# Block boundaries of a three-layer transformer kernel: transposing x before its norm, and projecting one token tile at a time

## The chip, the cores and the metric

The kernel runs on one core of a Trainium2 chip. The metric is the device time of one execution, in microseconds (us): the median of several runs. Five engines work side by side, each through its own instructions in order, and wait for each other by semaphores: TensorE (PE in the profile) multiplies matrices and writes to PSUM, VectorE (DVE) and ScalarE (ACT) work element by element, GpSimd (POOL) does little here, and SyncE (SP) issues the loads.

## The reference, cut to what matters

The input x has 256 tokens of 1024 features, in fp32. Two layers (an even and an odd one) come first, each a mixer and an MLP, and then one hybrid layer.

```python
def rmsnorm(x, g):
    y = xf * lax.rsqrt(jnp.mean(xf * xf, axis=-1, keepdims=True) + EPS)
    return (y * g.astype(jnp.float32)).astype(x.dtype)

def sq_relu_mlp(h, w1, w2):
    return jnp.square(jax.nn.relu(h @ w1)) @ w2

    for l in range(DEPTH):                       # DEPTH = 2
        h = rmsnorm(x, g[0])
        y = even_mixer(...) if l % 2 == 0 else odd_mixer(...)     # each begins with h @ w_in
        x = x + rmsnorm(y, g[1])
        h = rmsnorm(x, g[2])
        x = x + rmsnorm(sq_relu_mlp(h, mlp_w1[l], mlp_w2[l]), g[3])

    # hybrid layer: first operations
    shift, scale, gate = jnp.split(jax.nn.silu(c) @ w_ada + b_ada, 3, axis=-1)
    h = rms_norm(x, g_pre) * (1 + scale[:, None, :]) + shift[:, None, :]
    ... = jnp.split(h @ w_in, cuts, axis=-1)
```

So there are four places where one block's output passes through an rmsnorm, is added to x, and x passes through the next rmsnorm (with a bias at the fourth) into the next block's first projection. They are called boundaries here: 1 before the first MLP, 2 before the odd mixer, 3 before the second MLP, 4 before the hybrid layer.

## The kernel before

Everything is held in SBUF except the weights, which stream through in 150 tiles of 1 MB (128 partitions x 2048 fp32). `plan_tiles` lists them in the order of use. SyncE loads each into one of three buffers `raw`; a buffer is loaded again once its tile has been split. Each tile is split into two parts of a reduced fp32 format, so that three fast matmuls give an fp32 product: ScalarE casts it to `w_hi` (line 968) and VectorE writes the rest, `raw - w_hi`, to `w_lo` (line 1322). Three slots of `w_hi`/`w_lo` hold split tiles; a slot is taken again when TensorE has used its tile. Activations are split in the same way: `h_hi`/`h_lo` for a normed input, `f_hi`/`f_lo` for the inner MLP activation. TensorE's lines 464 to 466 are the three products.

The order of every engine's work is the order in which its program is written. ScalarE and VectorE run ahead of TensorE by a count: `split_until(past(name, 2))` (or `ahead(name)`) means "split all tiles up to two beyond this group, then go on". Six tiles per MLP (`ada`) are not split but summed on VectorE with a per-partition factor (lines 1313 to 1317), in place of their split.

Projections from x come in two kinds. Feature-major (`project_feature_major`): a stationary block of the weights, the moving operand `h` of 256 tokens, output with features on the partitions, 96 matmuls of 128x256 for one group of 512 columns. Token-major (`project_token_major`): `h` is stationary. Outputs go to one of two PSUM pairs `lin0`/`lin1` (1024 columns each), which take turns by a list (`plan_lin`). Row-wise sums (the last matmul of a block) go to `acc` (2048 columns: two token tiles of 1024 features). Of these sums the last two weight tiles are done together, token tile 0 first.

At a boundary `residual` runs on ScalarE and VectorE after `split_until(LAST[name] + 1)`, one token tile of 128 tokens at a time: ScalarE squares the block's output (line 987) and takes the root (983); VectorE takes the mean (1339), multiplies by the gain row (1380), takes the reciprocal (1343) and updates x (1387). Then ScalarE squares the new x, takes the root, and VectorE scales an identity matrix by 1/norm (1349). TensorE turns x by a matmul of x with that diagonal (`norm_in`, line 553), so that x is transposed and normed at once. When both token tiles are turned, `to_h` multiplies by the gain: ScalarE writes `h_hi` (1008) and VectorE `h_lo` (1361, with a bias 1364 and 1365) in pieces of 128x256, and the first projection starts.

After boundaries 1 and 3 the MLP's first projection `up_0` is read by ScalarE (relu, line 1029), squared on ScalarE (1033, `f_hi`) and VectorE (1586, 1588, `f_lo`), while TensorE does `up_1`; then `down_0` is summed. After boundary 2 the first projection `mq` is copied (1089) and passes through a four-tap convolution on VectorE (1625, 1627), and a small projection `mrowg` of gate rows feeds a chain of small operations (1656 to 1665). After boundary 4 `dk` goes the same way: copy, convolution, silu (1144), square (1205), and then a sum on TensorE (767).

## Time and profile before

| | us |
|---|---|
| median of 3 runs | 1030.27 (1027.41 to 1030.48) |
| span of the profiled execution | 1026.5 |
| TensorE busy | 953.2 (93%) |
| VectorE busy | 632.9 (62%) |
| ScalarE busy | 495.2 (48%) |
| loaded from HBM | 163.60 MB, 160 GB/s over the span |

The span is what the profiler saw from the first to the last instruction. The execution's own time is not listed apart from the three runs; they are 0.9 to 4.0 us above the span. A median 3.8 us above the span is the relation used below.

How to read the rows further down: a row of a timeline gives the start (us from the span's start), the duration of the merged piece, the engine, the line of the kernel, the operation and its operands with their shapes, and in brackets the idle time before it and whose result ended that idle time. "PE" rows overlap, since matmuls are pipelined: 128x256 matmuls that last 0.28 start 0.12 apart, 128x512 ones 0.23 apart.

### The profile page before, as it was taken

The page shows a single profiled execution, that of the slowest core. Times are in us where ns is not written, and L with a number is a line of the kernel's source. Part 1 is how long each engine was busy: PE and PEld are TensorE (multiplying, and loading weights), DVE is VectorE, ACT ScalarE, POOL GpSimd, SP SyncE. Part 2 cuts the span into 40 slices and gives each one's busy share as a digit, 9 for nine tenths or more (in the row PEclk, how much of TensorE's full clock was granted, in tenths as well). Part 3 has the DMA queues.
Part 4 walks back from the last instruction along what each step waited for, and adds up shares of the span by engine and source line. Part 5 has one row for each costly group of instructions (what it writes and reads, how often), then busy time and mean ns, then how long its engine had stood idle before and what let it go on. Part 6 is the DMA issues. An engine that isn't in the chain of part 4 may idle for free.

```text
span 1026.5 us, 13530 instructions
## 1 busy us (share of the span) xinstructions
PE 953.2 (93%) x5794; PEld 853.5 (83%) x5794; DVE 632.9 (62%) x738; ACT 495.2 (48%) x604; POOL 28.0 (3%) x21
## 2 busy tenths in 40 slices
PE   6999978989999997998889999999799999989897
PEld 6998867789999996976769999998698998877776
DVE  4678644667656656685557666655758673345655
ACT  6554534564444445435545444444555743237433
POOL 0000000000000000000000000000000232100000
PEclk9999989999999999998898999999799899999999
DMA  8545412536666543343334765665233242222431
GB/s 327 186 165 188 147 75 82 205 145 259 233 220 232 205 164 144 129 159 135 111 141 147 281 232 205 237 242 180 87 137 111 96 164 80 85 103 83 164 124 41
DMA packets 23755, 165.51 MB, mean 161 GB/s; under 512 B 2640, under 2 KB 2896, under 8 KB 4368
## 3 DMA queue, kind: packets, MB, share of 16 engines
q1 hardware_dynamic: 22176, 159.39, 42.6%
q0 software_dynamic: 1088, 4.46, 1.1%
q8 instruction: 45, 0.74, 0.3%
q10 hardware_dynamic: 432, 0.81, 0.2%
q14 instruction: 14, 0.11, 0.0%
HBM read 163.60 MB, written 1.05 MB: 160 GB/s over the span
## 4 chain that ended last, share of the span: by engine, by line
PE 64%; DVE 14%; ACT 7%; issue 2%; DVEq 0%; ACTq 0%
PE lin L464 11%; PE lin L465 11%; PE lin L466 11%; PE acc L464 7%; PE acc L465 7%; PE acc L466 7%; DVE w_lo L1322 3%; PE acc L571 2%; DVE arena L1627 1%; ACT arena L987 1%; ACT w_hi L968 1%; PE acc L846 1%; PE acc L843 1%; DVE h_lo L1361 1%; PE acc L834 1%
## 5 line engine op out<-in xcount | busy, mean ns | idle before, releaser
L1322 DVE TENSOR_TENSOR w_lo<-raw,w_hi 128x2048 fp32r<-128x2048 f32 x138 | 318.1, 2317 | 147.5 <-ACT w_hi L968 147.1
L968 ACT CAST w_hi<-raw 128x2048 fp32r<-128x2048 f32 x138 | 261.8, 1906 | 175.7 <-PE lin L466 96.8
L464 PE MATMUL lin<-h_hi,w_hi 128*128 128x256 f32 x864 | 252.2, 292 | 11.4 <-DVE h_lo L1361 5.9
L465 PE MATMUL lin<-h_lo,w_hi 128*128 128x256 f32 x864 | 250.1, 289 | 0.0
L466 PE MATMUL lin<-h_hi,w_lo 128*128 128x256 f32 x864 | 249.9, 289 | 0.0
L464 PEld LDWEIGHTS lin<-h_hi,w_hi 128*128 128x128 f32 x864 | 171.6, 199 | 13.5 <-DVE h_lo L1361 6.9
L465 PEld LDWEIGHTS lin<-h_lo,w_hi 128*128 128x128 f32 x864 | 172.0, 199 | 0.4
L466 PEld LDWEIGHTS lin<-h_hi,w_lo 128*128 128x128 f32 x864 | 171.6, 199 | 0.0
L464 PE MATMUL lin<-w_hi,h_hi 128*128 128x512 f32 x272 | 110.1, 405 | 6.4 <-DVE h_lo L1361 2.7
L464 PE MATMUL acc<-w_hi,f_hi 128*128 128x512 f32 x288 | 112.4, 390 | 0.9 <-DVE w_lo L1322 0.9
L465 PE MATMUL acc<-w_lo,f_hi 128*128 128x512 f32 x288 | 112.2, 390 | 0.0
L466 PE MATMUL acc<-w_hi,f_lo 128*128 128x512 f32 x288 | 112.1, 389 | 0.0
L465 PE MATMUL lin<-w_lo,h_hi 128*128 128x512 f32 x272 | 107.3, 395 | 0.0
L466 PE MATMUL lin<-w_hi,h_lo 128*128 128x512 f32 x272 | 107.1, 394 | 0.0
L464 PEld LDWEIGHTS lin<-w_hi,h_hi 128*128 128x128 f32 x272 | 52.1, 191 | 18.5 <-issue 4.6
L464 PEld LDWEIGHTS acc<-w_hi,f_hi 128*128 128x128 f32 x288 | 54.1, 188 | 12.5 <-issue 1.7
L466 PEld LDWEIGHTS acc<-w_hi,f_lo 128*128 128x128 f32 x288 | 54.1, 188 | 11.4
L465 PEld LDWEIGHTS acc<-w_lo,f_hi 128*128 128x128 f32 x288 | 54.1, 188 | 10.6
L466 PEld LDWEIGHTS lin<-w_hi,h_lo 128*128 128x128 f32 x272 | 51.9, 191 | 11.3
L465 PEld LDWEIGHTS lin<-w_lo,h_hi 128*128 128x128 f32 x272 | 52.0, 191 | 10.0
L1089 ACT ACTIVATE arena<-lin 128x1024 f32<-128x1024 f32 x23 | 23.6, 1025 | 55.3 <-PE lin L466 55.2
L464 PE MATMUL acc<-w_hi,h_hi 128*128 128x512 f32 x112 | 44.2, 395 | 2.6 <-DVE arena L1538 1.6
(295 smaller groups left out, 1092.6 us busy)
## 6 DMA issues: line engine op xcount, KB each, us to landing
raw<-in_weights SPq DMA_DIRECT2D x150, 1024.0 KB, 4.8
rowbuf<-in_rows POOLq DMA_DIRECT2D x6, 512.0 KB, 3.8
x<-in_x_in SPq DMA_DIRECT2D x2, 512.0 KB, 4.5
arena<-in_const_even POOLq DMA_DIRECT2D x1, 1024.0 KB, 11.0
out<-x SPq DMA_DIRECT2D x2, 512.0 KB, 2.6
cst<-in_const ACTq DMA_DIRECT2D x1, 576.0 KB, 9.3
msk<-in_masks POOLq DMA_DIRECT2D x1, 256.0 KB, 6.8
colbuf<-in_cols ACTq DMA_DIRECT2D x1, 151.0 KB, 5.8
```

What stands on the lines that cost most here:

```text
L464: pe.matmul(dst, st_hi, mv_hi, start=first, stop=False)
L465: pe.matmul(dst, st_hi, mv_lo, start=False, stop=False)
L466: return pe.matmul(dst, st_lo, mv_hi, start=False, stop=last)
L571: mm = pe.matmul(dst[:, at:at + width], pt(h, s, t), v(h, s), start=(s == 0), stop=(s == t))
L834: mm = pe.matmul(acc[:, i * P:(i + 1) * P], at("am", P, (l % 2) * 1024 + i * P), at("X", P, i * P), start=True, stop=True)
L843: pe.matmul(acc[:, 1024 + i * P:1024 + (i + 1) * P], at("Y", P, i * P), at("Pm", P, i * P), start=True, stop=True)
L846: mm = pe.matmul(acc[:, i * P:(i + 1) * P], at("Pm", P, i * P), at("Y", P, i * P), start=True, stop=True)
L968: act.copy(w_hi[:, o % SPLIT, :], raw[:, j % RAW, :]).then_inc(hi_done, 1)
L987: act.activation(arena[:, at:at + 512], src, ACT.Square, accum_out=stat[:, 2 * t + c:2 * t + c + 1]).then_inc(ss_ready, 1)
L1089: act.activation(dst.rearrange("p (t c) -> p t c", t=TT) if len(dst.shape) == 2 else dst, pair(name)[:, :].rearrange("p (t c) -> p t c", t ...
L1322: dve.tensor_tensor(w_lo[:, o % SPLIT, :], r, w_hi[:, o % SPLIT, :].bitcast(F32), ALU.subtract).then_inc(tile_split, 1)
L1361: ins = dve.scalar_tensor_tensor(lo, src, gain(k), hi, ALU.mult, ALU.subtract)
```

## The change

1. **x is transposed unscaled.** The 16 matmuls with the scaled diagonal (`norm_in`) go. TensorE transposes x itself (`turned`), four 128x128 pieces after each half of the update of x. Those of token tile 0 stand ahead of the last six matmuls of the block's sum (`between`; not at boundary 4), which for token tile 1 is done tile by tile instead of column half by column half.
2. **The norm factor follows the projection.** At boundaries 1 to 3 `h` is x times the gain only. The projection's output is multiplied by 1/norm when it is read: as ScalarE's `scale` for token-major outputs, and for feature-major ones by a row of factors on all partitions (`every`), made by one matmul of ones with a diagonal (line 656 of the new kernel). The MLP's relu of `up_1` to `up_7` moves from ScalarE to VectorE for that. At boundary 4, which has a bias, x is scaled by VectorE before the transpose.
3. **The first projection is token-major, one token tile at a time** (`lead`): 96 matmuls of 128x256 into `acc`, each token tile as soon as its `h` is there. ScalarE reads it (`lead_out`), and TensorE transposes it back with eight 128x128 transposes (`lead_turned`), in the MLP in the middle of `up_1`, else after the small gate projection.
4. **Two more slots for split tiles** in the free part of the work area, for the MLPs' tiles and `mq`, `dk` (`plan_slots`), and three tiles instead of one are split ahead of the boundary's own work (`split_until(past(name, 3))`).
5. `h` is written in pieces of 128x128 (one token tile) instead of 128x256.

```diff
+            def lead(name, names, done, scaled=False):
+                def products(i, t, ks):
+                    hi, lo = split_tile(FIRST[name] + i)
+                    at = t * 512 + i * 256
+                    for k in ks:
+                        if i == 0 and k == 0:
+                            after(ht_ready)
+                        if i == 0 and k == 4:
+                            read_out(pe, names[t])
+                        w = slice(k * 256, (k + 1) * 256)
+                        st = [part[:, k, t * P:(t + 1) * P] for part in (h_hi, h_lo)]
+                        mm = passes(acc[:, at:at + 256], *st, hi[:, w], lo[:, w], k == 0, k == DC - 1)
+                    return mm
...
+                    products(0, 0, range(8))
+                    turned(1, 0, names, done)
+                    products(1, 0, range(4))
+                    turned(1, 1, names, done)
+                products(1, 0, range(4, 8)).then_inc(lead_done, 1)
+                products(0, 1, range(8)).then_inc(tile_used, 1)
+                if not scaled:
+                    after(rd_ready)
+                    pe.matmul(acc[:, 1024:1024 + T], ones, arena[:, LEAD["diag"]:LEAD["diag"] + T],
+                              start=True, stop=True).then_inc(rb_done, 1)
+                products(1, 1, range(8)).then_inc(tile_used, 1)
...
             def mlp(l):
-                project_feature_major(f"up{l}_0")
+                lead(f"up{l}_0", (f"n{l}c0", f"n{l}c1"), 2 * l)
                 for i in range(8):
-                    if i < 7:
+                    if i == 0:
+                        project_feature_major(f"up{l}_1", (0,))
+                        lead_turned(f"up{l}_0")
+                        project_feature_major(f"up{l}_1", (1,))
+                        after(r_ready)
+                    elif i < 7:
                         project_feature_major(f"up{l}_{i + 1}")
                     after(f_ready)
...
-            norm_in(["n1a", "n1b"])
-            project_feature_major("mq")
+            lead("mq", ("n1a0", "n1a1"), 1)
             gate_rows("mrowg")
+            lead_turned("mq")
             project_feature_major("mk")
...
+            # ScalarE
+            def boundary(name, names, gain, bias=None):
+                split_until(past(name, 3))
+                for c in range(2):
+                    sum_squares(name, 0, c)
+                tile_root(0)
+                x_squares(0)
+                sum_squares(name, 1, 0)
+                x_root(0)
+                h_part(0, 0)
+                if bias is None:
+                    h_part(0, 1)
+                    sum_squares(name, 1, 1)
+                    tile_root(1)
+                    h_part(1, 0)
+                    h_part(1, 1)
+                    x_squares(1)
+                    x_root(1)
...
+            # VectorE
+                split_until(past(name, 3))
+                after(s_row, 16)
+                after(ss_ready)
+                row_gain(0, 0, row)
+                tile_root(0, lambda: row_gain(0, 1, row))
+                updated(0)
+                x_mean(0)
+                after(ss_ready)
+                row_gain(1, 0, row)
+                x_scale(0)
+                h_part(0, 0)
+                if bias is None:
+                    h_part(0, 1)
+                    tile_root(1, lambda: row_gain(1, 1, row))
+                    updated(1)
+                    h_part(1, 0)
+                    h_part(1, 1)
...
+            # VectorE, odd mixer: mk is scaled here instead of copied by ScalarE
+            dve.tensor_tensor(pre.rearrange("p (c t) -> p c t", c=4), pair("mk")[:, :].rearrange("p (c t) -> p c t", c=4), every,
+                              ALU.mult).then_inc(freed("mk"), 1)
```

Three places show how the order moves. First VectorE ahead of boundary 2, where the last sum of the first MLP ends: the rows are splits of weight tiles (`w_lo<-raw,w_hi`, and `x_lo<-raw,x_hi` for the new slots) and then the first gain of the boundary. Before:

```order
L1406 TENSOR_TENSOR h_lo<-colbuf,h_hi 128x8x4
L1322 TENSOR_TENSOR w_lo<-raw,w_hi 128x2048 [waits hi_done] x3
L1380 TENSOR_TENSOR arena<-acc,rowbuf 128x512 [waits ss_ready,row_loaded]
L1339 TENSOR_SCALAR stat<-stat 128x1 [waits ss_ready,dve_step]
L1380 TENSOR_TENSOR arena<-acc,rowbuf 128x512
```

Now:

```order
L1673 TENSOR_TENSOR h_lo<-colbuf,h_hi 128x8x4
L1505 TENSOR_TENSOR x_lo0_51<-raw,x_hi0_49 128x2048 [waits hi_done]
L1505 TENSOR_TENSOR x_lo1_52<-raw,x_hi1_50 128x2048 [waits hi_done]
L1505 TENSOR_TENSOR w_lo<-raw,w_hi 128x2048 [waits hi_done] x3
L1563 TENSOR_TENSOR arena<-acc,rowbuf 128x512 [waits ss_ready,row_loaded]
L1521 TENSOR_SCALAR stat<-stat 128x1 [waits ss_ready,dve_step]
```

Five splits stand ahead of the boundary's first operation instead of three.

Second, TensorE at boundary 2, around the first projection `mq` (only the first row of each three products is shown). Before:

```order
L553 MATMUL lin0<-arena,x 128x128 [waits lin_free0,xn_ready]
L553 MATMUL lin0<-arena,x 128x128 x3
L553 MATMUL lin1<-arena,x 128x128 [waits lin_free1]
L553 MATMUL lin1<-arena,x 128x128 x3
L553 MATMUL lin0<-arena,x 128x128 [waits xn_ready]
L553 MATMUL lin0<-arena,x 128x128 x3
L553 MATMUL lin1<-arena,x 128x128 x4
```

Now:

```order
L622 MATMUL lin0<-cst,x 128x128 [waits lin_free0,x_done]
L622 MATMUL lin0<-cst,x 128x128 x3
L622 MATMUL lin0<-cst,x 128x128 [waits x_done]
L622 MATMUL lin0<-cst,x 128x128 x3
...
L507 MATMUL acc<-w_hi,h_hi 128x256 [waits ht_ready,tile_split]
...
L507 MATMUL acc<-w_hi,h_hi 128x256 [waits lin_free0]
...
L622 MATMUL lin1<-cst,x 128x128 [waits lin_free1,x_done]
L622 MATMUL lin1<-cst,x 128x128 x3
L507 MATMUL acc<-w_hi,h_hi 128x256 [waits tile_split]
```

The transposes wait for x alone, the first products for the `h` of one token tile, and token tile 1 is turned among them.

Third, VectorE at the start of the first MLP: the square of `up_0` (`arena<-arena`), its low part `f_lo`, the sum over an `ada` tile, and the splits of the two tiles of `down_0`. Before:

```order
L1322 TENSOR_TENSOR w_lo<-raw,w_hi 128x2048 [waits hi_done] x2
L1586 TENSOR_TENSOR arena<-arena 128x1024 [waits lin_free1]
L1588 TENSOR_TENSOR f_lo<-arena,f_hi 128x1024 [waits f_hi_ready,dve_step]
L1313 TENSOR_SCALAR ada_acc<-raw,stat 128x512 [waits loaded0]
L1315 SCALAR_TENSOR_TENSOR ada_acc<-raw,stat,ada_acc 128x512 [waits dve_step] x2
L1317 SCALAR_TENSOR_TENSOR ada_acc<-raw,stat,ada_acc 128x512 [waits dve_step]
L1322 TENSOR_TENSOR w_lo<-raw,w_hi 128x2048 [waits hi_done,tile_split]
```

Now:

```order
L1505 TENSOR_TENSOR w_lo<-raw,w_hi 128x2048 [waits hi_done,c_ready]
L1861 TENSOR_TENSOR arena<-arena 128x1024 [waits lin_free0,r_ready]
L1863 TENSOR_TENSOR f_lo<-arena,f_hi 128x1024 [waits f_hi_ready,dve_step]
L1495 TENSOR_SCALAR ada_acc<-raw,stat 128x512 [waits loaded0]
L1497 SCALAR_TENSOR_TENSOR ada_acc<-raw,stat,ada_acc 128x512 [waits dve_step] x2
L1499 SCALAR_TENSOR_TENSOR ada_acc<-raw,stat,ada_acc 128x512 [waits dve_step]
L1505 TENSOR_TENSOR w_lo<-raw,w_hi 128x2048 [waits hi_done,tile_split]
```

The order is the same, but the square now waits for a projection that has been turned back in the middle of `up_1`.

## Rows read from the trace of the kernel before

**Rows 1.** The page's first part: busy time, share of the span, instructions
```profile
PE 953.2 (93%) x5794; PEld 853.5 (83%) x5794; DVE 632.9 (62%) x738; ACT 495.2 (48%) x604; POOL 28.0 (3%) x21
```
**Rows 2.** Timeline of TensorE at boundaries 1 to 4, idle before in brackets
```profile
210.85 3.33 PE L553 MATMUL lin<-arena,x 128*128 128x128 f32 x16 [3.34 <-DVE arena L1349]
215.19 0.36 PE L464 MATMUL lin<-h_hi,w_hi 128*128 128x256 f32 x1 [1.01 <-DVE h_lo L1361]
...
399.22 2.05 PE L553 MATMUL lin<-arena,x 128*128 128x128 f32 x16 [0.40 <-DVE arena L1349]
404.32 2.05 PE L553 MATMUL lin<-arena,x 128*128 128x128 f32 x16 [3.05 <-DVE arena L1349]
408.20 0.35 PE L464 MATMUL lin<-h_hi,w_hi 128*128 128x256 f32 x1 [1.82 <-DVE h_lo L1361]
...
541.72 0.55 PE L464 MATMUL lin<-h_hi,w_hi 128*128 128x256 f32 x1 [1.17 <-DVE h_lo L1361]
...
735.35 0.55 PE L464 MATMUL lin<-h_hi,w_hi 128*128 128x256 f32 x1 [3.27 <-DVE h_lo L1365]
```
**Rows 3.** Windows of TensorE: busy time, instructions, granted clock, DMA share, GB/s
```profile
238.00:372.00 134.00, 134.00 (x863) 1.00 0.65 234
...
410.00:412.00 2.00, 2.00 (x11) 0.50 0.00 0
...
740.00:742.00 2.00, 2.00 (x11) 0.50 0.00 0
```
**Rows 4.** Timeline of ScalarE at boundary 2
```profile
381.08 3.71 ACT L968 CAST w_hi<-raw 128x2048 fp32r<-128x2048 f32 x2
...
390.70 0.60 ACT L987 ACTIVATE arena<-acc 128x512 f32<-128x512 f32 x1 [1.90 <-PE acc L466]
...
396.71 0.63 ACT L987 ACTIVATE arena<-x 128x512 f32<-128x512 f32 x1 [1.08 <-DVE x L1387]
...
405.52 3.02 ACT L1008 ACTIVATE h_hi<-lin,colbuf 128x256 fp32r<-128x256 f32 x8 [1.77 <-PE lin L553]
...
421.46 1.02 ACT L1089 ACTIVATE arena<-lin 128x1024 f32<-128x1024 f32 x1 [3.81 <-PE lin L466]
```
**Rows 5.** Timeline of VectorE at boundary 2
```profile
383.02 4.49 DVE L1322 TENSOR_TENSOR w_lo<-raw,w_hi 128x2048 fp32r<-128x2048 f32 x2 [1.52 <-ACT w_hi L968]
...
394.22 0.21 DVE L1339 TENSOR_SCALAR stat<-stat 128x1 f32<-128x1 f32 x1 [2.03 <-ACT arena L987]
...
395.93 1.41 DVE L1387 SCALAR_TENSOR_TENSOR x<-arena,stat,x 128x512 f32<-128x512 f32 x2
...
406.39 3.23 DVE L1361 SCALAR_TENSOR_TENSOR h_lo<-lin,colbuf,h_hi 128x256 fp32r<-128x256 f32 x8 [2.06 <-ACT h_hi L1008]
```
**Rows 6.** The page's DMA issues: count, KB each, median us to landing
```profile
raw<-in_weights SPq DMA_DIRECT2D x150, 1024.0 KB, 4.8
```
**Rows 7.** Timeline of TensorE late in the kernel: eight transposes of 128x128
```profile
996.69 1.09 PE L540 MATMUL lin<-cst,arena 128*128 128x128 f32 x8 [1.70 <-DVE arena L1878]
```
**Rows 8.** Timelines of ScalarE, VectorE and TensorE at the first MLP's start
```profile
227.19 1.02 ACT L1029 ACTIVATE arena<-lin 128x1024 f32<-128x1024 f32 x1 [3.79 <-PE lin L466]
...
228.25 1.23 DVE L1586 TENSOR_TENSOR arena<-arena 128x1024 f32<-128x1024 f32 x1 [2.52 <-ACT arena L1029]
...
233.53 4.49 DVE L1322 TENSOR_TENSOR w_lo<-raw,w_hi 128x2048 fp32r<-128x2048 f32 x2
...
238.51 0.40 PE L464 MATMUL acc<-w_hi,f_hi 128*128 128x512 f32 x1
```
**Rows 9.** Timeline of VectorE in the odd mixer
```profile
422.52 1.14 DVE L1625 TENSOR_SCALAR arena<-arena,colbuf 128x256 f32<-128x256 f32 x4 [2.54 <-ACT arena L1089]
...
437.74 0.28 DVE L1656 TENSOR_SCALAR arena<-arena 4x256 f32<-4x256 f32 x1 [0.92 <-ACT arena L1158]
```
**Rows 10.** Timelines of ScalarE and TensorE after boundary 4
```profile
751.45 1.02 ACT L1089 ACTIVATE arena<-lin 128x1024 f32<-128x1024 f32 x1 [3.81 <-PE lin L466]
...
761.26 0.94 PE L767 MATMUL acc<-cst,arena 128*128 128x1 f32 x7 [1.21 <-ACT arena L1205]
```

More of the change, by code:

```diff
@@ L125, in ada_summed, with plan_slots @@
     return f"ada{j}" if i % 2 == 1 and i < 6 and j < 4 else None
+def plan_slots():
+    mlp = {"mlp_w1_0", "mlp_w2_0", "mlp_w1_1", "mlp_w2_1"}
+    slots, free, opened = [], {}, set()
+    for n, t in enumerate(TILES):
+        if is_ada(n):
+            continue
+        o = ORDINAL[n]
+        roomy = t[2] in mlp or t[0] in ("mq", "dk")
+        slot = min(range(SPLIT + EXTRA if roomy else SPLIT), key=lambda i: free.get(i, i - SPLIT - EXTRA))
+        until = ("y0c" if t[2].endswith("_0") else "y1b") if slot >= SPLIT and t[2] in mlp else None
+        slots.append((slot, free.get(slot, -1), None if (slot, until) in opened else until))
+        opened.add((slot, until))
+        free[slot] = o
+    return slots
+SLOTS = plan_slots()
 def plan_lin():
@@ L132, in mlp @@
     def mlp(l):
-        out = [f"*n{l}c", f"*n{l}d", f"up{l}_0"]
+        out = [f"n{l}c0", f"n{l}c1"]
         for i in range(8):
@@ L494, in project_token_major, with accumulate_rows @@
                         mm.then_inc(tile_used, 1)
-            def accumulate_rows(name, part_of, first, last, before={}):
+            def accumulate_rows(name, part_of, first, last, before={}, between=None):
                 n0, n1 = FIRST[name], LAST[name]
@@ L711, in _ @@
             after(rows_ready)
+            after(r_ready)
             to_columns((7, 9))
```

372 lines of the change are left out of this document (261 added, 111 removed).

## The prediction, made before the changed kernel ran

> **What bounds the kernel now.** I read the page's first part first: TensorE is busy for 953.2 us, 93% of the span of 1026.5 [rows 1]. So the time is TensorE's work plus its pauses. The windows of the MLP between 238 and 372 us show 134 us busy of 134 at a granted clock of 1.00 [rows 3]: nothing is to be won there. The timeline of TensorE at the boundaries shows the pauses [rows 2]. At boundary 2 it turns token tile 0 at 399.22, pauses 3.05 us, turns tile 1 at 404.32, pauses 1.82 and starts `mq` at 408.20. Boundary 1 is alike (3.34 and 1.01), boundary 3 ends in 1.17, and boundary 4 ends in a pause of 3.27, since the bias doubles VectorE's operations. After the pauses the granted clock is 0.50, that is 1.2 instead of 2.4 GHz, at 410 to 412 and at 740 to 742 [rows 3]. From the end of a block's sum to the end of the next projection pass 22.6 us at boundary 2 (0.40 before 399.22, so from 398.8, to the copy at 421.46 [rows 2, 4]), of which the projection needs 12.0 (215.19 to 227.19 at boundary 1 [rows 2, 8]).
>
> **The lead itself.** TensorE's work hardly changes. The matmuls with the diagonal go, 2.05 us per token tile [rows 2]; sixteen transposes come, 1.09 for eight [rows 7], and eight more to turn the result back. The matmul for the factors is 128x256 in fp32, about 0.5 by the 0.40 of a 128x512 fast one [rows 8], with 0.2 to 1.0 as ends. Sum 3 x 1.09 + 0.5 - 2 x 2.05 = -0.3 us per boundary. The gain must come from the pauses.
>
> **The splits ahead of the boundary.** I follow boundary 2. ScalarE casts weight tiles from 381.08, 1.86 each [rows 4], VectorE splits them from 383.02, 2.25 each [rows 5]. Before, three tiles stand ahead of the first square at 390.70, now five. Two are loaded. Buffers are three, so the fourth tile's load can begin only when the first split ends (385.3), and lands 4.8 us later [rows 6], at 390.1; the fifth's begins at 387.5 and lands at 392.3. Cast 394.2, split 396.5. Then come a gain (0.7), mean and root (0.4), the second gain (0.7): x is updated from 398.4, where it was 395.93 [rows 5]. So token tile 0 is late by 2.5 us at boundary 2; at 1 and 3 the same count gives about 1.7 and 1.5, at 4 half a us, as its loads start earlier. Ends: 0, if the casts fit into ScalarE's idle time, and 3. TensorE reaches the transposes six matmuls before its old end, at 398.8 - 6 x 0.23 = 397.4, and must wait for x until 399.1: the wait is new, and the six matmuls queue behind it.
>
> **From x to the first products.** After the first half of x: two squares of x (1.4, from the 0.63 of one [rows 4]), one square of the block's output (0.6), the root (0.2), four casts and four subtractions of 128x128. Eight casts of 128x256 take 3.02 us and one 128x512 square 0.60 [rows 4]; the slope gives 0.29 for 128 columns. Eight subtractions take 3.23 us, a 128x512 update 0.70 [rows 5], so 0.28. Four and four: 2.3. With the waits between the engines I take 4.75 in all: first products at 399.1 + 4.75 = 403.9. The Trainium skill speaks against the finer pieces here: "VectorE: DVE Perf Modes", section on the TRN2 errata, says that every operation pays a fixed latency and recommends tiles of 512 elements or more. Its table (172 and 120 fixed cycles from PSUM) would give 0.25 and 0.26 us for 128 columns, so 0.2 us less per boundary than my rows; the finer pieces cost some 0.2 us each beyond their share, and the sum does not hang on it.
>
> **The lead's end.** 96 matmuls at 0.12 (11.5 to 12.0 by boundary 1), eight transposes 1.1, the factors 0.5: 13.1 us without a further pause, since token tile 1's x is ready 2.9 us after the start, when the first 24 products end. `mq` ends at 417.0 instead of 421.46, 4.4 earlier; at boundary 1 at 222.6 instead of 227.19, at 3 about 5 us earlier. A fully freed pause would be 2 to 3 us better.
>
> **What is late next.** This decides, because the result must be turned back.
>
> - *MLP start (boundaries 1 and 3).* Before, ScalarE reads `up_0` at 227.19, VectorE squares from 228.25, does `f_lo`, sums an `ada` tile, and begins the split of `down_0` at 233.53; its first tile is ready at 235.8, 8.7 us after `up_0` ended. TensorE comes for it at 238.51 [rows 8]: 2.7 us of slack. Now the same chain starts after half of `up_1` (5.8) and eight transposes (1.1), 6.9 us after the lead's end. So `down_0` can start 6.9 + 8.7 + 0.1 = 15.7 us after the lead: 222.6 + 15.7 = 238.3. TensorE is through with `up_1` at 235.3 and pauses 3.0 us. Gain: 0.2 to 0.5 us at boundary 1, 0.7 at 3, in place of 4.6 and 5.
> - *Odd mixer (2).* VectorE's convolution starts at 422.52 and the gate rows at 437.74 [rows 9]; this engine's chain, not TensorE, ends last until the scores. Now the lead ends at 417.0, less 0.4 from before, the gate projection takes 2.9, the turning back 1.1, the copy 1.0, and ScalarE first does two tanh: the convolution starts at 422.4. The gate rows gain 1.1, as they no longer wait for `mk`; scaling `mk` costs VectorE 1.2. Sum 0, ends -2 and +2.
> - *Hybrid layer (4).* `dk` ends at 751.45 and the sum over squares starts at 761.26 [rows 10]. Now x is scaled (0.7), turned, cast, and with the bias takes four more VectorE operations per half; TensorE has pauses of 2.5, 3.3, 1.8, 0.8, 1.8 and 1.0 within. I get 747.5 for the end at full clock; but this stretch ran at a clock of 0.50 before, as at 740 to 742 [rows 3], and TensorE's work is no denser in it now; I add 2 for that: 749.5. Then gate projection, turning back, the two sigmoid rows ahead of the copy, convolution (6.2), silu and square: 13.8 us, so 763.3 instead of 761.26. Cost 2.0, ends 0 and 5.
> - *Clock.* A pause of 3.05 and one of 3.34 were each followed by half clock [rows 2, 3]. Such a stretch costs TensorE about 1.7 us (410 to 412 and its neighbours). I take one after each MLP start: +3.4, ends 0 and 3.4. In the leads at 1 to 3 the pauses are cut to about 2 and 2, and I take full clock.
>
> Moving the relu to VectorE costs nothing: it has 38% idle, and its 1.2 us take the place of a wait for ScalarE of 2.52 [rows 8]; without that cover it would be 14 x 1.2. The two slots give nothing in the MLP, where TensorE never waits.
>
> **The sum.** -0.4 - 0 - 0.7 + 2.0 + 3.4 = +4.3. The span becomes 1030.8; the median lay 3.8 above the span, so 1034.6.
>
> **Rivals.**
>
> - *Clock kept.* No half clock follows the two 3.0 us pauses: 1034.6 - 3.4 = 1031.2. For it: after a pause of 1.70 the eight transposes still took 1.09, full speed [rows 7]; against: this one is as long as those that did. Chance 0.30.
> - *Faster: the early splits do not hold up x.* If ScalarE and VectorE get tiles four and five done before the first square can begin anyway, each of three leads ends about 2.2 us earlier, and 6.6 us come back on top of the kept clock: 1031.2 - 6.6 = 1024.6. It decides at boundary 2: x updated before 396.5. Against: three buffers and 4.8 us per load [rows 6]. Chance 0.18.
> - *Faster: all that the leads save survives.* VectorE's chain is not what ends last. Then 4.6 + 4.4 + 5 + 2 less four times 1.1 is 11.6: 1018.7. The Trainium skill has this as its advice ("Perfetto Trace Analysis", "Optimizing Scalar/DVE Operations": breaking up instructions that cause bubbles on other engines lets work finish sooner). Against: the 2.7 us of slack in [rows 8]. Chance 0.07.
> - *Slower: half clock in the leads too.* Two pauses of some 2 us close together lower the clock as one long one did. Each of three leads loses 1.7, and `dk` runs wholly at half clock (3 more): 1034.6 + 8 = 1042.7. Chance 0.15.
>
> **Chances.** Forecast 0.30, clock kept 0.30, the faster two 0.25, the slow one 0.15. A measurement tells 0.3% (3.1 us) from no change. Slower by more than that: forecast and the slow one, 0.45. Within: 0.30. Faster: 0.25. The range leaves out the 1018.7 case and half of the slow one: 1023 to 1041. The forecast's own range is 1032 to 1037.
>
> **What would show it.** In the changed profile: x of token tile 0 at boundary 2 updated near 398.4 from the span's start, shifted by what came before; the lead's first products about 4.8 us later; TensorE waiting about 3 us for the split of `down_0` in both MLPs, with granted clock 0.50 after it; the sum after `dk` near 763. I am wrong if TensorE enters `down_0` without a wait, or if x is updated within half a us of the last acc column's square.

## The result, and the profile after

| | before | changed |
|---|---|---|
| median | 1029.04 us (1027.41 to 1030.48, 4 runs) | 1040.66 us (1035.60 to 1041.23, 4 runs) |
| span of the profiled execution | 1026.5 | 1038.7 |
| ratio of the times | | 1.0112 (95% interval 1.0080 to 1.0144) |

The change makes the kernel slower by 1.1%, 11.6 us by the medians. Measured a second time beside other kernels it gave 1038.27 against 1028.75 us, ratio 1.0102 (1.0072 to 1.0132). The direction was as predicted and 1040.66 lies just inside the range of 1023 to 1041, but the move is more than twice the +4.3 us of the forecast.

The page of the changed kernel, the engines' busy time and the weight loads:

```profile
PE 954.0 (92%) x5768; PEld 848.5 (82%) x5768; DVE 654.6 (63%) x795; ACT 488.1 (47%) x635; POOL 28.1 (3%) x21
...
raw<-in_weights SPq DMA_DIRECT2D x150, 1024.0 KB, 4.9
```

TensorE works as long as before, 954.0 against 953.2 us [rows 1]. Since a matmul at half clock counts as longer work, this says that the 12 us are pauses: TensorE's idle time, span less busy time, rose from 73.3 to 84.7 us. A second trace of each kind says the same: 83.9 us idle in the changed kernel, 73.1 in a kernel that differs from the one before by two early casts and is as fast. Half clock is found in both kernels, and as much of it: the mean granted clock was 0.966 in ten executions of the changed kernel and 0.967 in 57 of the kernel before. The change has only moved it.

The timeline of TensorE shows the pauses, at the places of [rows 2, 8, 10]:

```profile
205.54 1.32 PE L622 MATMUL lin<-cst,x 128*128 128x128 f32 x8 [1.57 <-DVE x L1568]
209.91 0.36 PE L507 MATMUL acc<-x_hi,h_hi 128*128 128x256 f32 x1 [1.67 <-DVE h_lo L1623]
238.34 0.77 PE L507 MATMUL acc<-w_hi,f_hi 128*128 128x512 f32 x1 [3.13 <-DVE w_lo L1505]
...
402.75 1.97 PE L622 MATMUL lin<-cst,x 128*128 128x128 f32 x8 [3.01 <-DVE x L1568]
407.12 0.36 PE L507 MATMUL acc<-w_hi,h_hi 128*128 128x256 f32 x1 [0.59 <-DVE h_lo L1623]
...
457.93 0.79 PE L507 MATMUL lin<-w_hi,h_hi 128*128 128x512 f32 x1 [8.68 <-DVE arena L1945]
...
537.77 1.63 PE L622 MATMUL lin<-cst,x 128*128 128x128 f32 x8 [1.96 <-DVE x L1568]
570.56 0.77 PE L507 MATMUL acc<-w_hi,f_hi 128*128 128x512 f32 x1 [3.13 <-DVE w_lo L1505]
...
734.87 1.09 PE L622 MATMUL lin<-cst,arena 128*128 128x128 f32 x8 [3.40 <-DVE arena L1601]
...
771.24 3.57 PE L881 MATMUL acc<-cst,arena 128*128 128x1 f32 x16 [3.76 <-ACT arena L1390]
```

The reader sees four kinds of wait: for x ahead of the transposes (1.57, 3.01, 1.96, and 3.40 at boundary 4); for the split of `down_0` at both MLP starts (3.13, 3.13); a new one of 8.68 ahead of `mv1` in the odd mixer; and one of 3.76 ahead of the sum of squares (1.21 before). Windows of TensorE (busy time, instructions, granted clock, DMA share, GB/s) show what follows them:

```profile
238.00:240.00 2.00, 1.66 (x4) 0.56 1.01 422
240.00:242.00 2.00, 2.00 (x6) 0.58 1.01 418
...
572.00:574.00 2.00, 2.00 (x6) 0.50 1.00 406
574.00:576.00 2.00, 2.00 (x6) 0.50 1.01 401
```

After both waits of 3.13 the granted clock is about 0.5, the 1.2 GHz level, and TensorE does 6 instead of 10 matmuls in two microseconds. It is not always so: six traces here have the two waits of 3.13 unchanged, and in ten of these twelve places half clock follows, in two it does not.

Set side by side, the same matmul in both traces gives where the time went. The shift is the start in the changed kernel less the start before.

| up to | changed | before | shift | of this stage | forecast |
|---|---|---|---|---|---|
| first matmul of `down_0`, MLP 1 | 238.34 | 238.51 | -0.2 | -0.2 | -0.4 |
| start of the last sum of that MLP | 389.74 | 387.66 | +2.1 | +2.3 | +1.7 |
| second sum tile of the odd mixer | 526.01 | 521.20 | +4.8 | +2.7 | 0 |
| first matmul of `down_0`, MLP 2 | 570.56 | 566.65 | +3.9 | -0.9 | -0.7 |
| last matmul of that MLP | 731.07 | 723.63 | +7.4 | +3.5 | +1.7 |
| sum of squares after `dk` | 771.24 | 761.26 | +10.0 | +2.6 | +2.0 |
| eight late transposes | 1008.88 | 996.69 | +12.2 | +2.2 | 0 |

Counted between the same places, TensorE's idle time grew by 2.2, 0.2, 2.8, 0.7, 0, 5.2 and 0.4 us, row by row: the pauses were added ahead of the MLPs, in the odd mixer and above all at boundary 4.

One trace holds such a table only to 1 to 3 us a row. Executions of one kernel differ by where the clock happens to be low: a second profiled execution of the changed kernel had a span of 1032.9, not 1038.7, with the same waits, and entered `down_0` of MLP 1 at 235.04. So what follows rests on medians of several executions, and on waits that every trace shows. The profiled execution of the changed kernel took 1040.46 us, 1.8 more than its span, and not the 3.8 that the forecast added. In the executions of the kernel before whose own span is known the difference is 1.8 to 2.5 us.

### The profile page after: what moved, and what is told of

Read it like the earlier page. It is cut to its first block, busy times and chain, and to the rows that moved or that the text cites. A ratio compares the mean times of both kernels' runs of the same rounds, so it can differ in the third digit from the quotient of the medians.

```text
span 1038.7 us, 13568 instructions
## 1 busy us (share of the span) xinstructions
PE 954.0 (92%) x5768; PEld 848.5 (82%) x5768; DVE 654.6 (63%) x795; ACT 488.1 (47%) x635; POOL 28.1 (3%) x21
## 4 chain that ended last, share of the span: by engine, by line
PE 58%; DVE 17%; ACT 8%; DMA 2%; issue 2%; DVEq 0%; ACTq 0%
PE lin L507 9%; PE lin L509 9%; PE lin L508 9%; PE acc L507 7%; PE acc L509 7%; PE acc L508 7%; DVE w_lo L1505 4%; DMA raw<-in_weights 2%; ACT w_hi L1084 2%; PE acc L683 2%; DVE arena L1899 1%; PE acc L960 1%; ACT arena L1194 1%; DVE arena L1563 1%; DVE x_lo L1505 1%
## 5 line engine op out<-in xcount | busy, mean ns | idle before, releaser
L1505 DVE TENSOR_TENSOR w_lo<-raw,w_hi 128x2048 fp32r<-128x2048 f32 x110 | 252.4, 2308 | 96.3 <-ACT w_hi L1084 95.6
L507 PE MATMUL lin<-h_hi,w_hi 128*128 128x256 f32 x576 | 166.3, 289 | 3.7 <-DVE h_lo L1551 1.9
L508 PE MATMUL lin<-h_lo,w_hi 128*128 128x256 f32 x576 | 164.9, 286 | 0.0
L509 PE MATMUL lin<-h_hi,w_lo 128*128 128x256 f32 x576 | 164.8, 286 | 0.0
L507 PEld LDWEIGHTS lin<-h_hi,w_hi 128*128 128x128 f32 x576 | 112.4, 195 | 4.8 <-DVE h_lo L1551 2.0
L508 PEld LDWEIGHTS lin<-h_lo,w_hi 128*128 128x128 f32 x576 | 112.6, 195 | 0.2
L1505 DVE TENSOR_TENSOR x_lo<-raw,x_hi 128x2048 fp32r<-128x2048 f32 x28 | 63.7, 2289 | 17.2 <-ACT x_hi L1084 17.2
L507 PE MATMUL acc<-w_hi,h_hi 128*128 128x512 f32 (+1 forms) x176 | 64.8, 368 | 9.6 <-DVE h_lo L1625 6.2
L509 PE MATMUL acc<-w_hi,h_lo 128*128 128x512 f32 (+1 forms) x176 | 62.9, 357 | 0.0
L508 PE MATMUL acc<-w_lo,h_hi 128*128 128x512 f32 (+1 forms) x176 | 62.9, 357 | 0.0
```

Of the source, the lines that this page charges most:

```text
L507: pe.matmul(dst, st_hi, mv_hi, start=first, stop=False)
L508: pe.matmul(dst, st_hi, mv_lo, start=False, stop=False)
L509: return pe.matmul(dst, st_lo, mv_hi, start=False, stop=last)
L1505: dve.tensor_tensor(lo, r, hi.bitcast(F32), ALU.subtract).then_inc(tile_split, 1)
```

## Experiments

All are edits of the changed kernel except one. "Ratio" is to the kernel before on the same chip; the changed kernel stands at 1.0112 and 1.0102, on average 1.0107, and 0.001 is 1.03 us.

| | median, us | ratio to before (95%) | against the changed kernel |
|---|---|---|---|
| MLP start: splits ahead of the squares | 1028.61 | 0.9998 (0.9981 to 1.0014) | -11.2 us |
| `mk` copied at once | 1038.43 | 1.0096 (1.0074 to 1.0118) | -1.1 |
| two tiles ahead of the boundaries | 1027.39 | 0.9990 (0.9970 to 1.0010) | -12.0 |
| boundary 4 as before | 1031.79 | 1.0023 (1.0002 to 1.0043) | -8.6 |
| MLP pauses filled | 1036.71, 1036.13 | 1.0095 (1.0062 to 1.0129), 1.0087 (1.0055 to 1.0119) | -1.2, -1.5 |
| casts ahead of the silu | 1035.34 | 1.0073 (1.0051 to 1.0095) | -3.5 |
| four edits together | 1014.10 | 0.9862 (0.9822 to 0.9902) | -25.2 |
| and boundary 4 as before | 1011.28 | 0.9836 (0.9801 to 0.9870) | -27.9 |
| and three waits filled | 1011.33 | 0.9836 (0.9802 to 0.9870) | -27.9 |
| kernel before, casts ahead of the silu | 1027.75 | 0.9997 (0.9974 to 1.0020) | |

### The start of the MLP

```diff
 # ScalarE, and the same on VectorE ahead of the loop
                 lead_out(f"up{l}_0", 1, ACT.Relu)
+                split_until(past(f"up{l}_0", 3))
                 for i in range(8):
```

> The changed kernel with one edit: at the start of each MLP, ScalarE casts and VectorE splits the first tile of down_0 (and VectorE sums the ada tile ahead of it) while TensorE does the first half of up_1, that is before the copy and the squares of up_0, not after them. My theory: the wait of 3.13 us for that split and the one stretch of half clock behind it are the whole cost of the MLP starts, so each MLP gets 3.1 + 1.7 us shorter: 9.6 us in all, 1040.7 - 9.6 = 1031. The granted clock stays 1.00 at 238 to 242. Rival A (absorbed): at boundaries 2 and 4 token tile 0's x waits for weight tiles whose loads set the pace, so what the MLP saves is waited out there: half of it or less is left, 1036 to 1038. Rival B (VectorE is full): TensorE waits elsewhere in the MLP, 1040.

Measured: 1028.61 us, ratio 0.9998, level with the kernel before. The timeline of VectorE in the new order, in the first MLP:

```profile
222.47 2.29 DVE L1506 TENSOR_TENSOR w_lo<-raw,w_hi 128x2048 fp32r<-128x2048 f32 x1 [3.62 <-ACT w_hi L1084]
...
227.55 2.29 DVE L1506 TENSOR_TENSOR w_lo<-raw,w_hi 128x2048 fp32r<-128x2048 f32 x1
230.69 1.22 DVE L1863 TENSOR_TENSOR arena<-arena 128x1024 f32<-128x1024 f32 x1 [0.85 <-ACT arena L1212]
```

The `ada` sum and the split of `down_0` (227.55) now stand in what was an idle time of 6 us, the square still starts at 230.69 (230.62 in the changed kernel), and TensorE enters `down_0` at 235.20 without a wait. At the last sum of the first MLP 4.8 us are saved (384.96 against 389.74), as expected, and by the medians 11.2 in all where 9.6 were expected; rivals A and B fall. So the 3.13 us were no law of the data flow: the squares never needed to come first.

### The wait of 8.68 us in the odd mixer

```diff
 # ScalarE
-            ahead("mk")
+            copy_out("mk", arena[:, O_AT["pre"] + 1024:O_AT["pre"] + 2048])
 # VectorE: scales the copy in place, instead of reading PSUM
```

> The changed kernel with one edit: ScalarE copies mk out of PSUM as soon as it is done (as before the change), and VectorE scales the copy in place later. TensorE's new wait of 8.68 us ahead of mv1 must go. My theory: VectorE's chain (convolution of mq, gate rows, convolution of mk) ends last in the odd mixer, and the long wait only stands where the wait of 3.85 us ahead of the sums stood, which comes back: the time changes by 0, at most by one stretch of half clock (-1.7): 1039 to 1041, and the second convolution starts at the same time within 0.5 us. Rival: the wait costs what it is long, less the 3.85: 1036 or less.

Measured: 1038.43 us, ratio 1.0096; the intervals of this and of the changed kernel overlap. The waits of TensorE and the end of VectorE's chain:

```profile
451.49 0.76 PE L507 MATMUL lin<-w_hi,h_hi 128*128 128x512 f32 x1 [2.11 <-DVE w_lo L1505]
470.37 1.19 PE L838 MATMUL acc<-arena 128*128 128x256 f32 x2 [3.65 <-DVE stat L1950]
...
457.92 1.14 DVE L1897 TENSOR_SCALAR arena<-arena,colbuf 128x256 f32<-128x256 f32 x4
```

The longest new wait in the kernel is gone and the time hardly moves. The second convolution starts at 457.92, where it started at 457.91 with the wait, and a wait of 3.65 us ahead of the scores has come back. By the medians 1.1 of the 8.68 us were a cost, and that lies within the error: `mk` keeps its PSUM pair until VectorE has scaled it, TensorE waits for that, and would else wait for the same chain a little later.

### How many tiles are split ahead of a boundary

```diff
 # ScalarE and VectorE, boundary
-                split_until(past(name, 3))
+                split_until(past(name, 2))
 ...
                     x_root(1)          # VectorE: x_scale(1)
+                    split_until(past(name, 3))
```

> The changed kernel with one edit: at the boundaries two tiles instead of three are split ahead of the boundary's own work, and the third after the norm factor of token tile 1. My theory: the last early split delays the update of x; token tile 0's x comes 2.3 to 3.7 us earlier at boundaries 1 to 3, TensorE's waits of 1.57, 3.01 and 1.96 us there fall to under 0.5, and the stretches of half clock behind two of them go: -6 to -8 us, 1033 to 1035. Rival A: x is held by the square of the block's output or by the fourth tile's load; the waits stay over 1 us and the time is 1038 to 1040. Rival B: what the leads gain ahead of the odd mixer is waited out by VectorE's splits there and the gain is that of the two MLP boundaries alone, -3 to -4: 1037.

Measured: 1027.39 us, ratio 0.9990: 12.0 us come back. First what the changed kernel does at boundary 2, in the timelines of ScalarE and VectorE that answer to [rows 4, 5]:

```profile
392.22 1.91 ACT L1084 CAST w_hi<-raw 128x2048 fp32r<-128x2048 f32 x1 [3.54 <-DMA raw<-in_weights]
396.03 1.91 ACT L1084 CAST w_hi<-raw 128x2048 fp32r<-128x2048 f32 x1 [1.90 <-DMA raw<-in_weights]
...
385.10 4.49 DVE L1505 TENSOR_TENSOR x_lo<-raw,x_hi 128x2048 fp32r<-128x2048 f32 x2 [1.51 <-ACT x_hi L1084]
...
397.98 2.29 DVE L1505 TENSOR_TENSOR w_lo<-raw,w_hi 128x2048 fp32r<-128x2048 f32 x1 [1.52 <-ACT w_hi L1084]
400.19 0.68 DVE L1563 TENSOR_TENSOR arena<-acc,rowbuf 128x512 f32<-128x512 f32 x1
...
401.94 1.42 DVE L1568 SCALAR_TENSOR_TENSOR x<-arena,stat,x 128x512 f32<-128x512 f32 x2
```

Both engines stand idle for a load, twice, with the sums of token tile 0 long ready in `acc`, and the update of x follows straight behind the last split. With one split fewer, VectorE and TensorE:

```profile
392.11 2.29 DVE L1506 TENSOR_TENSOR w_lo<-raw,w_hi 128x2048 fp32r<-128x2048 f32 x1 [2.34 <-ACT w_hi L1084]
...
396.08 1.41 DVE L1569 SCALAR_TENSOR_TENSOR x<-arena,stat,x 128x512 f32<-128x512 f32 x2
...
397.56 1.03 PE L622 MATMUL lin<-cst,x 128*128 128x128 f32 x8
401.25 0.35 PE L507 MATMUL acc<-w_hi,h_hi 128*128 128x256 f32 x1 [1.26 <-DVE h_lo L1624]
```

x comes 5.9 us earlier, of which 2.0 had been gained before this point (387.71 against 389.74 at the last sum), so 3.8 by the edit. At boundary 3 it is some 2.7, and the waits for x at the first three boundaries are gone. At boundary 1 the first products come at 206.64 and not at 209.91, but TensorE was also done 1.3 us sooner with what stands ahead, and a second trace of the changed kernel has them at 206.63; so 2.0 by the edit. That is 8.5 us at three boundaries; at boundary 4 the wait falls from 3.40 to 1.08. My theory holds with more than it claimed; rival A falls at all three, and rival B too: the odd mixer took over its 3.8 in full (432.23 against 438.09 at `mv0`). What these leads save comes through, as a shift of all that follows.

### Boundary 4 as before

```diff
 # TensorE
-            lead("dk", ("n2a0", "n2a1"), 3, True)
+            norm_in(["n2a", "n2b"], LEAD["diag"])
+            project_feature_major("dk")
             gate_rows("drowg")
-            lead_turned("dk")
 # ScalarE, VectorE: residual, to_h, copy of dk and sigmoids in the order of before
```

> The changed kernel with boundary 4 (before the hybrid layer) as before the change: x is turned by the scaled diagonal, dk is projected feature-major, one tile is split ahead. By the landmarks of the two traces the way from the end of the last MLP sum to the sum of squares takes 39.8 us in the changed kernel and 35.4 before: 4.4 us come back, and up to 2 more behind it if the clock in the hybrid layer follows as before: 1040.7 - 4.4 = 1036.3, down to 1034. Rival: my forecast's own price for this boundary, 2.0 us, was right and the rest is due to where the clock happened to be low: 1038.7.

Measured: 1031.79 us, ratio 1.0023, 8.6 us better than the changed kernel, twice what I expected. (The edit also takes away the third early split at this boundary.) The expectation also had a mistake in it: its 35.4 us of before are counted from the end of the first token tile's turn. From the last matmul of the sum it is 37.6 before (723.63 to 761.26) and 40.2 in the changed kernel (731.07 to 771.24): in this pair of traces the boundary itself costs 2.6, near the 2.0 of the forecast. TensorE in this run:

```profile
734.50 3.68 PE L605 MATMUL lin<-arena,x 128*128 128x128 f32 x16 [3.39 <-DVE arena L1548]
741.49 0.55 PE L507 MATMUL lin<-h_hi,w_hi 128*128 128x256 f32 x1 [3.31 <-DVE h_lo L1564]
...
765.24 1.95 PE L881 MATMUL acc<-cst,arena 128*128 128x1 f32 x16 [1.21 <-ACT arena L1396]
```

Ahead of the sum of squares it waits 1.21 us, not 3.76, and the sixteen matmuls take 1.95, not 3.57. In the changed kernel the granted clock falls there:

```profile
772.00:774.00 2.00, 2.00 (x11) 0.50 0.00 0
774.00:776.00 2.00, 2.00 (x10) 0.50 0.00 0
```

and in this run it stays up:

```profile
766.00:768.00 2.00, 2.00 (x19) 1.00 0.00 0
```

All nine traces with the new path at this boundary, the changed kernel's two among them, have the wait of some 3.8 us and half clock behind it for 7 to 11 us; of the five with the old path three have 3 to 4 us of half clock there and two have none. From the sum of squares on to the transposes at 829 (841 in the changed kernel) this run is 5.2 us shorter (64.7 against 69.9). That is as short as the old path gets. Over all traces this stretch takes 69.9 to 70.3 us with the new path and 64.7 to 67.8 with the old one, and the stretch ahead of it, from the last matmul of the sum, 39.3 to 42.6 in the seven with the new path and three early splits, 36.3 to 37.7 with the old. So the new boundary costs some 3 to 4 us on its own stretch and 2 to 5 behind it. The mean granted clock of the ten executions of this run is 0.971, against 0.966 for the changed kernel; TensorE's idle time is 3.8 us less (80.9 against 84.7).

### Filling the pause of the MLP start

```diff
                         after(r_ready)
+                        for j in range(12):
+                            pe.matmul(acc[:, 1536:2048], h_hi[:, 0, 0:P],
+                                      h_hi[:, 2 * (j % 4):2 * (j % 4) + 2, :], start=True, stop=True)
                     elif i < 7:
```

> The changed kernel with twelve matmuls of 128x512 added in TensorE's wait of 3.13 us ahead of down_0 in each MLP (products of h_hi with itself into the part of acc that the next matmul of the sum overwrites; they change no result). They take 12 x 0.23 = 2.8 us, so the wait stays as long as before but TensorE works in it. Theory: the half clock behind the wait is set off by the pause, so the granted clock stays 1.00 behind it and each MLP gets 1.7 us shorter: 1040.7 - 3.4 = 1037.3. Rival (the low clock comes by itself, or the added work prolongs the path): 1040 or more.

> The changed kernel itself, so that the next run has it on the same chip: ratio to before 1.008 to 1.014 as measured.

> The changed kernel with twelve matmuls added in each wait ahead of down_0, once more, beside the changed kernel. The trace of the first time shows the granted clock kept at 1.00 behind both. Theory: 1.7 us less per MLP comes through to the end: ratio to before lower by 0.0033 than the changed kernel's, some 3.4 us. Rival: at boundaries 2 and 3 the fifth early split waits for its load, and takes back what the MLP gained: lower by less than 0.0015.

Measured: 1.0095, then 1.0087 beside a changed kernel at 1.0102. TensorE's waits and windows in the first of the two:

```profile
239.16 0.47 PE L507 MATMUL acc<-w_hi,f_hi 128*128 128x512 f32 x1 [0.38 <-DVE w_lo L1507]
571.85 0.47 PE L507 MATMUL acc<-w_hi,f_hi 128*128 128x512 f32 x1 [0.38 <-DVE w_lo L1507]
...
240.00:242.00 2.00, 2.00 (x11) 1.00 1.00 414
...
574.00:576.00 2.00, 2.00 (x10) 1.00 0.98 414
```

With the pause filled with work of no use, the granted clock stays at 1.00, in both MLPs and both times. Unfilled, the same wait was followed by half clock in ten of twelve places. One of the two others is the first MLP of the run with the casts ahead of the silu, which comes further down:

```profile
238.10 0.47 PE L507 MATMUL acc<-w_hi,f_hi 128*128 128x512 f32 x1 [3.13 <-DVE w_lo L1506]
240.00:242.00 2.00, 2.00 (x10) 1.00 1.00 426
```

So the idle time has a large part in setting off the half clock, but four places against two exceptions in twelve do not show that it is the whole cause; what else decides is not shown. The pair also gives the price: this MLP takes 149.8 us from the first matmul of `down_0` to the last sum, as with the pause filled (149.8, 149.9), and 151.4 in the changed kernel, so 1.6 us for the stretch of half clock. In time, 1.2 and 1.5 us less than the changed kernel's ratio were measured where 3.4 were expected, with intervals that overlap by most of their width. It is not settled how much came through. One trace shows a way to lose it: at boundary 3 the fifth split's load was waited for 1.5 us longer, and x with it:

```profile
539.07 1.33 PE L622 MATMUL lin<-cst,x 128*128 128x128 f32 x5 [3.46 <-DVE x L1570]
```

against 1.96 in the changed kernel.

### VectorE's chain in the odd mixer

```diff
             copy_out("mq", arena[:, O_AT["pre"]:O_AT["pre"] + 1024])
+            ahead("mk")
             conv_silu(O_AT["q"], ("convb", 0))
```

> The changed kernel with one edit in the odd mixer: ScalarE casts the two tiles of mv0 while VectorE runs the convolution of mq, and does the silu of mq after them, not before. VectorE then finds them cast when the convolution ends and does not wait 3.56 us. Theory: VectorE's chain sets the end of the odd mixer's scores; all of it from the splits at 435.66 on is 3.5 us earlier, and so is the time: 1037.2. Rival: something else (TensorE's projections of v, the loads) ends last and less than 1 us comes through: 1040.

> The kernel before with the one edit of the odd mixer alone: ScalarE's casts of mv0 ahead of the silu of mq. Theory: nothing comes through, since there the gate rows (437.74) wait for ScalarE's tanh, and these for the copy of mk at 435.86, not for the splits: the same time within 1 us, ratio 0.999 to 1.001. The 3.5 us that this edit gives in the changed kernel are then a gain that the change made possible. Rival: VectorE's chain moves as in the changed kernel: 3.5 us less, 0.9965.

Measured: in the changed kernel 1.0073, 3.5 us less; in the kernel before 0.9997, nothing. VectorE in the changed kernel, what answers to [rows 9] and the wait in question, and then the same with the casts first:

```profile
425.85 0.35 DVE L1897 TENSOR_SCALAR arena<-arena,colbuf 128x256 f32<-128x256 f32 x1 [1.88 <-ACT arena L1271]
...
435.66 4.49 DVE L1505 TENSOR_TENSOR w_lo<-raw,w_hi 128x2048 fp32r<-128x2048 f32 x2 [3.56 <-ACT w_hi L1084]
440.07 0.28 DVE L1931 TENSOR_SCALAR arena<-arena 4x256 f32<-4x256 f32 x1
```

```profile
425.15 5.07 DVE L1900 SCALAR_TENSOR_TENSOR arena<-arena,colbuf 128x255 f32<-128x255 f32 x12
430.14 4.48 DVE L1506 TENSOR_TENSOR w_lo<-raw,w_hi 128x2048 fp32r<-128x2048 f32 x2
434.55 0.28 DVE L1932 TENSOR_SCALAR arena<-arena 4x256 f32<-4x256 f32 x1
```

The splits follow the convolution without the 3.56 us, and all behind them is earlier by that. In the kernel before the splits are earlier too, but the gate rows wait for ScalarE's tanh, which stands behind the copy of `mk`:

```profile
438.60 0.28 DVE L1657 TENSOR_SCALAR arena<-arena 4x256 f32<-4x256 f32 x1 [3.36 <-ACT arena L1159]
```

Since the changed kernel does the tanh ahead of `mq`, this wait of 3.56 us is the last one there. By this the change had opened 3.5 us that it did not collect.

### Together

> The changed kernel with four edits: the split of down_0 ahead of the squares (as in the run where the MLP starts are reordered), two tiles instead of three ahead of the boundaries, ScalarE's casts ahead of the silu and its early copy of mk in the odd mixer. Theory: the savings add, as each removes another wait: 11.2 + 11.3 + 3.5 from the landmarks, less one or two stretches of half clock that the first two both counted: 1015 to 1019, below the kernel before. Rival: with the leads earlier, VectorE no longer gets through its splits and TensorE waits in the MLP: 1023 or more.

> The same four edits, and boundary 4 as before the change. Theory: another 5.6 us up to the sum of squares, and what the clock gives behind it: 1009 to 1014. Rival: the fourth boundary's price was that of its third early split, which is gone already: the same time as the run with the four edits within 2 us.

> The fastest kernel so far (four edits and the old boundary 4) with matmuls that change no result in three of its waits: 24 of 128x128 in the wait of 3.39 us ahead of the second token tile at boundary 4, 12 of 128x512 in the wait of 3.29 us ahead of dk, 14 of 128x512 in the wait of 3.65 us in the odd mixer. Theory: three stretches of half clock go, 1.7 us each, as far as TensorE sets the pace behind them: ratio 0.9836 - 0.0045 = 0.979, down to 0.977. Rival: behind these places VectorE's chain sets the pace, so the clock is kept and the time stays at 0.9836.

The four edits give 1014.10 us, ratio 0.9862, 25.2 less than the changed kernel; the single edits sum to 11.2 + 12.0 + 3.5 + 1.1 = 27.8. They add almost fully. Which of the five parts of the change brings the gain over the kernel before was not tested. With the old boundary 4 it is 1011.28, ratio 0.9836 (0.9801 to 0.9870), 1.6% faster than the kernel before, and the fastest measured here, level with the same kernel with three waits filled. Its 2.8 us over the four edits lie within the intervals; by the traces the stretch from the last matmul of the sum to the sum of squares is 37.9 us in the one and 37.7 in the other (40.2 in the changed kernel), so on that stretch the third early split was the price, as the rival said, and what is left of the difference lies behind it (70.0 against 67.4 us up to the transposes).

The last run had matmuls of no use in three waits, and gained nothing. In the wait ahead of the second token tile at boundary 4 I had counted 24 matmuls of 0.13 us; the timeline shows 48 records, 5.5 us for a wait of 3.4:

```profile
707.21 1.95 PE L610 MATMUL lin<-arena,x 128*128 128x128 f32 x16
708.99 5.52 PE L602 MATMUL lin<-arena,x 128*128 128x128 f32 x48
714.35 1.95 PE L610 MATMUL lin<-arena,x 128*128 128x128 f32 x16
```

The clock stayed at 1.00 from 710 to 726, where it had been near 0.5 for most of 10 us, and the filling took back the 2 us that this gave. In the odd mixer 1.85 us of wait were left over, and half clock followed from 457 to 461 all the same. Whether a filling of the right length would pay is open.

## Why the prediction was right, and where it was too small

**The leads and the MLP starts were right, the pause to the tenth.** Forecast: `down_0` at 238.3 after a pause of 3.0; measured 238.34 and 3.13. The pause is the same in every trace with that order; the place is luck in part, as the second trace has 235.04. From the first half of x to the first products 4.75 forecast, 4.5 measured at both boundary 1 and 2 (from 205.44 and 402.65, half an update behind 204.74 and 401.94). Pieces of 128x128: eight take 2.16 us on both engines, 0.27 each where I had 0.29 and 0.28 (a straight line through my rows gives 0.27 and 0.26, so I had drawn it wrongly). In the trace they start 0.25 us apart on ScalarE and 0.26 on VectorE. The Trainium skill ("VectorE: DVE Perf Modes", section on the TRN2 errata) gives 0.25 and 0.26, and the trace agrees. Lead 13.1 forecast, 13.0 measured. That the savings of the lead would be waited out by VectorE's work on `down_0` was the core of the forecast, and the first experiment shows it: reorder that work and 11.2 us come back (forecast for the two pauses and what follows them: 9.4).

**The term of half clock was of the right size, but half clock is not what made the kernel slow.** I took 1.7 us behind each MLP pause. The first MLP took 2.3 us more than before: 1.6 for half clock, 0.2 for a longer wait, and 0.5 that I did not look for. The second took 3.5 more, since there the clock stayed low for 7 us: 2.7 for that, and 0.8 that it also shows in traces without half clock (157.8 against 157.0). Over the twelve such places in six traces, the two without it included, half clock costs 1.6 us on average, so the last 1 us is where the clock happened to be low. In the leads I took full clock; the traces show half clock at boundary 2 (402 to 406) and 3 (538 to 542), in the second trace at 2 alone. That is part of the slower rival, 1042.7, which I gave 0.15, but not what it named: not two pauses of 2 us close together but one of 2 to 3 us for x. The number of that rival is nearest to the result, yet its cause fails: the mean granted clock is that of the kernel before (0.966 against 0.967), and what grew is idle time, by 11 us. The kernel before had more of its half clock at the boundaries; the changed one has a part of it in the MLPs.

**The early splits were mis-sized.** The step "Cast 394.2, split 396.5" took 4.8 us for each load. The fourth tile came on time: 390.1 forecast, 392.22 measured with the 2.1 us of shift. The fifth's buffer was free at 389.6 and its data came at 396.03, after 6.4 us. The windows of that time show the DMA engines fully busy (share 0.94 to 1.14 from 390 to 396, some 2.5 MB), with the loads of the fourth, fifth and sixth tile under way together; I had given each load the 4.8 us of the median, whatever was under way beside it. Then x stood at 401.94 where the forecast with the shift is 400.5. At boundary 4 the step was wrong outright: half a us, "as its loads start earlier"; x is there at 730.36, 0.7 us ahead of the last matmul of the sum, where before it was 3.2 ahead (720.45 to 723.63), so 2.5 late. Taking the last split out gives 12.0 us by the medians, more than the forecast's own 6.2 for all that these splits delay. The rival in which they do not hold up x is thereby refuted: they hold it up at all four places.

**The odd mixer: 0 forecast, +2.7 in the traces.** The chain on VectorE was the right thing to look at, and its end (second convolution, 457.91 against 454.74) moved by 3.2, of which 2.1 came with the MLP: 1.1 in place of 0, inside the ends of -2 and +2. The rest is a longer half clock behind 504 (up to 512, before up to 505), so it may differ in another execution: the second trace of the changed kernel has this stage 1.0 us shorter. The wait of 8.68 us on `mk`'s pair I had not seen at all; it was harmless, as the second experiment shows.

**Boundary 4: 2.0 forecast, 5 to 6 by the traces and 8.6 by the medians.** For the stretch up to the sum of squares the number came out (763.3, with the shift 770.7; measured 771.24), but with luck. I had kept the half clock of before there. In fact TensorE's idle time grew by 5.2 us and half clock gave back 2.9 of them (low from 736 to 744, before from 730 to 744; an estimate from windows of 1 us). For what stands behind I forecast nothing, and the pair of traces has +2.2. The sum ended with the sum of squares. `dk` arrives late there, TensorE waits 3.76 us just ahead of dense work, and in all nine traces with that wait half clock follows. This is the largest single miss.

**Luck in the number.** 1034.6 contains 3.8 us between span and time, where the executions of the kernel before show 1.8 to 2.5 and those of the changed kernel 1.8: it is 1 to 2 us too high for this reason, and so are the ends of the range. With 1.8 the forecast would have been 1032.6 and the range would have ended at 1039, below the measured time. The upper end was also drawn through the middle of the slower rival, whose cause was not the one at work.

**The rivals.** "Clock kept" (1031.2) fails on the traces, and also in its price: with both MLP pauses filled and the clock kept the kernel still took 1036.71 and 1036.13 us. "All that the leads save survives" (1018.7, chance 0.07) was wrong for this change, yet right for its idea: with the three costs taken away the kernel comes to 1014.1. There the Trainium skill ("Perfetto Trace Analysis", section "Optimizing Scalar/DVE Operations") says that breaking up instructions that cause bubbles on other engines may let work finish sooner. The runs here say what has to come with it: the gain came through only when the order of the other work on ScalarE and VectorE was set by who waits for it.

## What to carry to other kernels

When a producer is made faster, list what stands ahead of the consumer's next need on every in-order engine, and move the work that nobody waits for behind the work that somebody does: three such moves were worth 11, 12 and 3.5 us here, with no operation added or removed. Work done early is not free on an engine in order, above all if it waits for a load. A long wait in a profile is not yet a cost: one of 8.68 us was worth about 1, within the error of the measurement, while two of 3.13 with half clock behind them were worth 11. And half clock that is plain to see after a change may have been there before, elsewhere: compare the mean granted clock and the idle time of both kernels before calling it the cause.

## What the runs showed of the hardware

- TensorE's granted clock went down behind idle time, though not each time. Behind a wait of 3.13 us it was about 0.5 in ten places of twelve; with twelve matmuls in that wait and 0.38 us left of it, it stayed at 1.00, four times out of four. A wait of 1.85 us in other surroundings was still followed by half clock.
- A stretch of half clock behind such a wait cost 1.6 us (151.4 against 149.8 for the same MLP), and 2.7 where it lasted 7 us.
- Of loads of 1 MB that overlap, one landed 4.9 us and the next 6.4 us after its buffer was free, with the DMA engines fully busy; the median over 150 is 4.9.
- An fp32 matmul of 128x128 stands in the trace as two records: 24 issued, 48 shown, 5.5 us in all. A transpose of 128x128 stands as one: eight issued, eight shown, 1.09 us.
